# Half-size weight slots with single-piece waits, and block products in three of the layers' input projections

## The reference, cut to what matters

```python
h = layer_norm(concat([meta, x]), ln_emb_g, ln_emb_b)        # 528 rows
for l in range(2):
    proj = h @ w_in[l]      # q,k,v,gate of retention; pool input; q,k,v of attention; forget logits
    mix = concat([retention(...), pool(...), forgetting_attention(...)]) @ w_out[l]
    h = layer_norm(ALPHA * h + mix, ln1_g[l], ln1_b[l])
    y = (silu(h @ w1[l]) * (h @ w3[l])) @ w2[l]              # inner width 2816
    h = layer_norm(ALPHA * h + y, ln2_g[l], ln2_b[l])
return h[16:]
```

## Time and profile before

| what | value |
|---|---|
| median of three runs | 3274.61 us (3264.3, 3274.61, 3277.98) |
| the profiled execution | 3272.24 us, span 3270.1 us |
| mean granted TensorE clock | 0.965 |
| busy share of TensorE, DVE, ACT | 94%, 36%, 17% |
| the two layers | from about 1735 us to the end |
| DMA busy share in slices of 82 us after 1735 us | 2 to 5 tenths |
| TensorE busy in the same slices | 8 to 9 tenths or more |

### The profile page before, as it was taken

One profiled execution on the slowest core, in us unless ns is written; L12 is line 12 of the kernel. 1 busy time (PEld: TensorE's weight loads), 2 busy tenths in 40 slices (PEclk: granted clock), 3 DMA queues, 4 the chain that ended last, 5 costly groups with the idle time before them and its releaser, 6 DMA issues.

```text
span 3270.1 us, 52738 instructions
## 1 busy us (share of the span) xinstructions
PE 3080.4 (94%) x22521; PEld 1730.5 (53%) x22521; DVE 1163.1 (36%) x2350; ACT 545.3 (17%) x1133; POOL 47.4 (1%) x58
## 2 busy tenths in 40 slices
PE   9878989799999999999989999998999989999999
PEld 3355545233333334333445668573786648675766
DVE  1633355222222222232363452527044342435131
ACT  1332320111111111111122221130112100130000
POOL 0000002000000000000010000000000000000000
PEclk9878989899999999999989999999999999999999
DMA  9800125899999999999853333324333243343442
GB/s 400 351 1 30 49 84 220 319 409 407 410 402 408 407 406 406 405 409 408 356 234 125 118 132 113 144 109 162 148 121 147 103 193 129 116 162 116 180 158 100
DMA packets 97467, 743.71 MB, mean 227 GB/s; under 512 B 11128, under 2 KB 38336, under 8 KB 57552
## 3 DMA queue, kind: packets, MB, share of 16 engines
q1 hardware_dynamic: 58768, 687.49, 53.1%
q10 hardware_dynamic: 32624, 30.52, 2.9%
q0 software_dynamic: 5968, 24.14, 1.9%
HBM read 674.98 MB, written 67.13 MB: 227 GB/s over the span
## 4 chain that ended last, share of the span: by engine, by line
PE 55%; DMA 26%; DVE 4%; ACT 2%; issue 1%; ACTq 1%; POOL 1%; DVEq 0%
DMA arena<-x_sorted 24%; PE psum L1648 19%; PE psum L1632 10%; PE psum L1577 5%; PE psum L1281 3%; PE psum L1588 3%; PE psum L1356 2%; PE psum L839 1%; PE psum L1392 1%; ACTq L597 1%; PE psum L1233 1%; PE psum L857 1%; PE psum L1679 1%; PE psum L1448 1%; DMA x_sorted<-arena 1%
## 5 line engine op out<-in xcount | busy, mean ns | idle before, releaser
L1281 PE MATMUL psum<-weight_ring,arena 128*32 128x512 f32 x6192 | 677.5, 595 | 42.8 <-DVE arena L2936 42.1
L1648 PE MATMUL psum<-arena,weight_ring 128*128 128x256 f32 (+1 forms) x2816 | 636.8, 385 | 5.7 <-ACT arena L2291 5.7
L1648 PEld LDWEIGHTS psum<-arena,weight_ring 128*128 128x128 f32 x2816 | 529.4, 190 | 102.2 <-issue 11.9
L1281 PEld LDWEIGHTS psum<-weight_ring,arena 128*32 128x32 f32 x6192 | 199.9, 110 | 500.7 <-issue 458.4
L1356 PE MATMUL psum<-weight_ring,arena 128*32 128x256 f32 x6144 | 338.2, 380 | 0.0
L1356 PEld LDWEIGHTS psum<-weight_ring,arena 128*32 128x32 f32 x6144 | 196.6, 110 | 153.0 <-issue 26.8
L2958 DVE STREAM_TRANSPOSE arena<-arena 128x384 f32<-128x384 f32 x32 | 18.6, 580 | 632.8 <-DMA arena<-x_sorted 632.8
L1632 PE MATMUL psum<-weight_ring 128*128 128x512 f32 x468 | 206.7, 600 | 10.1 <-DMA weight_ring<-weights 8.0
L3273 DVE TENSOR_TENSOR weight_ring<-weight_ring,psum 128x256 f32<-128x256 f32 (+1 forms) x88 | 37.4, 425 | 423.2 <-PE psum L1648 420.5
L1577 PE MATMUL psum<-weight_ring,arena 128*128 128x512 f32 (+2 forms) x512 | 175.0, 500 | 3.1 <-ACT arena L2291 3.1
L1632 PEld LDWEIGHTS psum<-weight_ring 128*128 128x128 f32 x468 | 89.5, 192 | 123.7 <-issue 118.6
(11 more groups left out here) (446 smaller groups left out, 2678.5 us busy)
## 6 DMA issues: line engine op xcount, KB each, us to landing
weight_ring<-exp_gu SPq DMA_DIRECT2D x129, 2048.0 KB, 11.6
weight_ring<-weights SPq DMA_DIRECT2D x104, 2048.0 KB, 7.9
weight_ring<-exp_down SPq DMA_DIRECT2D x64, 2048.0 KB, 11.1
x_sorted<-arena SPq DMA_DIRECT2D x2, 10752.0 KB
arena<-x_sorted ACTq DMA_DIRECT2D x132, 96.0 KB, 22.2
y_sorted<-arena ACTq DMA_DIRECT2D x128, 96.0 KB, 17.4
y_sorted<-arena SPq DMA_DIRECT2D x2, 5632.0 KB, 39.4
y_sorted<-arena SPq DMA_DIRECT2D x2, 5120.0 KB, 37.8
```

The costliest lines, as they stand in the source:

```text
L1281: mm = pe.matmul(psum[j * GROUP:(j + 1) * GROUP, g, :], xg[:, k // 4, g, k % 4 * GROUP:(k % 4 + 1) * GROUP], w[:, kk, j * 512:(j + 1) * 51 ...
L1648: mm = pe.matmul(bank[:, 0:b - a], w[:, k, col:col + P], h2_t[:, k, a:b], start=(k == 0), stop=(k == KT - 1))
```

## The change

The four slots of 2 MB become eight half slots of 1 MB. A piece of the projections, of `mix` and of `feed_up` takes two halves, a down chunk is now six pieces of one half each (three for the first 512 columns, three for the second, in an own input `down2`). A class `Piece` carries its landing wait and its releases, a class `Stream` finds which earlier pieces lay in the same halves. Block products wait on TensorE for single pieces inside p1 and release the second-column pieces after p3 and the last weight sums, the first-column pieces after p5.
The projections (0, A), (1, A) and (1, B) do row chunks 0 and 1 of the two full tiles as one block product, behind the meta items. ACT copies p1, p7, p6 and p3 to `u2`, DVE adds p2, p4 and p5, and ACT applies Silu to the gates in place at the end. The sums of rows go to the other half's columns of `h2_t`, so that the rows are kept.
The norms after `mix` become a generator (`mid_norms`): one tile at a time, between sums of the product or behind features. The norms after the second `feed_down` are centred for all tiles first and then scaled. The double steps of attention become fewer, and the steps inside `feed_down` go. ACT takes the last root of down (1, A) after the last turned tile instead of between the two.

```diff
+HALF_SLOTS, HALF = 2 * LAYER_SLOTS, PIECE // 2
-EARLY_STEPS = range(7, 18)
-DOUBLE_STEPS = dict(A=(4, 5, 6, 7, 8, 12), B=(5, 6, 7))
-DOWN_STEPS = (0, 2)
+EARLY_STEPS = range(4, 15)
+DOUBLE_STEPS = dict(A=(4, 5, 6), B=())
...
+class Stream:
+    def ask(self, source, size):
+        slot = self.at % HALF_SLOTS
+        self.arrived[slot] += 16
+        piece = Piece(source, self.at, size, self.ring[:, slot * HALF:(slot + size) * HALF], (self.landed[slot], self.arrived[slot]))
+        self.pieces.append(piece)
+        self.at += size
+        return piece
...
+        def rows_in_products(l, x):
+            return (l, x) != (0, "B")
...
-            for n in range(len(ROW_CHUNKS)):
+            if rows_in_products(l, x):
+                if x == "A":
+                    yield "meta", 0, 0
+                    yield "meta", 1, 0
+                yield "products", 1, WHOLE[x][-1]
+            for n in range(2 if rows_in_products(l, x) else 0, len(ROW_CHUNKS)):
...
             # TensorE, project
+                    if kind == "products":
+                        products(("product", l, x), KT // 2, left_blocks_kept(x), mix_blocks(ws), [ws[0]] * 2, [ws[1]], None, ("p1", "p7", "p6", "p3"))
+                        main.number["rows", l, x, n, t] = main.number["product", l, x, "p5"]
+                        continue
...
             # TensorE, products
+                        if n == 0 and name == "p1":
+                            first[part].wait(pe)
+                        if q == pairs - 1 and name == "p2" and left_whole is not None:
+                            left_whole(pe)
...
+                    main.ship(mm, (*key, name), "a" if name in copied else "v")
+                    if name == "p3":
+                        for piece in second:
+                            piece.free = [main.done(), (right_ready, parts + 4 * len(right))]
+                for piece in first:
+                    piece.free = [main.done()]
...
             # TensorE, feed_down
-                pe.wait_ge(*main.drained_of(("up", l, x, f1 - 1)))
-                ws = [weights(l, W_DOWN + 3 * c + n) for n in range(3)]
+                    second, first = ([down_weights(l, c, half, n) for n in range(DOWN_PIECES // 2)] for half in (1, 0))
...
+                    pe.wait_ge(*main.drained_of(("up", l, x, f1 - 2)))
+                    products(("down", l, x, c), pairs, left_blocks(ff_t, pairs, x, a), down_blocks(halves, c), first, second, last_ready)
...
             # ACT
+            def product_rows(l, x):
+                t1, t2 = WHOLE[x]
+                for name, t, at in (("p1", t1, 0), ("p7", t2, 512), ("p6", t2, 0), ("p3", t1, 512)):
+                    bank = main.take(act, ("product", l, x, name))
+                    A.did(act.copy(u2[:, t, at:at + 512], bank), main.drained["a"])
+                act.wait_ge(*main.drained_of(("product", l, x, "p5")))
+                gates = u2[:, t1:t2 + 1, U_G:2 * 512]
+                A.did(act.activation(gates, gates, ACT.Silu))
...
-                turn_rows("mid", 1, "B", (last,))
+                turn_rows("mid", 1, "B", (None, last))
...
             # DVE, project
+                    if kind == "products":
+                        ws = mark["rows", l, x]
+                        for w in ws:
+                            w.wait(dve)
+                        for before in range(2 if x == "A" else 0):
+                            main.take(dve, ("meta", l, x, before, 0))
+                        dve.wait_ge(*main.drained_of(("start", l, WHOLE[x][-1], 1)))
+                        products(("product", l, x), left_blocks_kept(x), mix_blocks(ws), x, u2,
+                                 copied_by=dict(p2="p1", p4="p6", p5="p3"), between=norms)
...
             # DVE, products
                 right_sums((0, 1), (1, 1), ALU.subtract, (0, 1))
-                V.did(dve.tensor_tensor(a21, a11, a21, ALU.subtract), left_ready)
+                left_sums("s3", "a11", ALU.subtract, "a21")
                 V.settle_other(left_ready)
-                V.did(dve.tensor_tensor(s2, a22, a21, ALU.subtract), left_ready)
+                left_sums("s2", "a22", ALU.subtract, "s3")
+                each(between)
                 gather("p1", t1, lo, scale, main.drained["v"])
...
             # DVE, mix and feed_down
+            def mid_norms(l, x):
                 for t in rows_of(l, x):
                     norm_rows(V, h2[0:SIZE[t], t, :], t, ln_par2, sem("mid_ready"), SIZE[t], first_half=(t == 0))
+                    yield
...
-                        for t in rows_of(l, x):
-                            norm_scaled(norm_centered(t), sem("layer_start"), parts)
+                        for both in [norm_centered(t) for t in rows_of(l, x)]:
+                            norm_scaled(both, sem("layer_start"), parts)
...
             # DVE, layers
-                project(0, "B", items=(SPLIT_B, 99))
+                project(0, "B", items=(SPLIT_B, 99), norms=mid_norms(0, "A"))
...
-                project(1, "A")
+                norms = mid_norms(0, "B")
+                each(norms)
+                project(1, "A", norms=norms)
...
-                project(1, "B")
+                norms = mid_norms(1, "A")
+                each(norms)
+                project(1, "B", norms=norms)
```

More of the change, by code:

```diff
@@ L414, in take, with __init__, wait, before @@
         return self.psum[:, self.at(self.taken - 1), :]
+class Piece:
+    def __init__(self, source, at, size, flat, landed):
+        self.source, self.at, self.size, self.flat, self.landed, self.free = source, at, size, flat, landed, []
+        self.rows = flat.rearrange("p (k n) -> p k n", n=512)
+    def wait(self, engine):
+        engine.wait_ge(*self.landed)
+class Stream:
+    def __init__(self, ring, landed):
+        self.ring, self.landed, self.arrived = ring, landed, [0] * HALF_SLOTS
+        self.pieces, self.at = [], 0
+    def ask(self, source, size):
+        slot = self.at % HALF_SLOTS
+        assert slot + size <= HALF_SLOTS
+        self.arrived[slot] += 16
[3 more added lines that the diff above has]
+        return piece
+    def before(self, piece):
+        places = {p % HALF_SLOTS for p in range(piece.at, piece.at + piece.size)}
+        found = []
+        for earlier in reversed(self.pieces[:self.pieces.index(piece)]):
+            own = {p % HALF_SLOTS for p in range(earlier.at, earlier.at + earlier.size)}
+            if own & places:
+                found.insert(0, earlier)
+                places -= own
+        return found
 def build(nc, io):
@@ L1548, in project @@
                 a, b = SPAN[x]
-                for number, (kind, n, t) in enumerate(project_items(x)):
+                ws = [weights(l, half) for half in range(2)] if rows_in_products(l, x) else []
+                mark["rows", l, x] = ws
+                for number, (kind, n, t) in enumerate(project_items(l, x)):
                     if not items[0] <= number < items[1]:
@@ L1597, in mix @@
                 pe.wait_ge(*fox_outs.drained_of(("fox", l, x, 3)))
-                ws, ats = zip(*(weights(l, W_OUT + half) for half in range(2)))
-                mark["mix", l, x] = ats
+                ws = [weights(l, W_OUT + half) for half in range(2)]
+                mark["mix", l, x] = ws
                 if 0 in rows_of(l, x):
@@ L1602, in mix @@
                         bank = main.bank(pe)
+                        ws[half].wait(pe)
                         for k in range(KT):
@@ L1640, in feed_up @@
                     if f % 2 == 0:
-                        w, at = weights(l, W_FFN + f // 2)
+                        piece = weights(l, W_FFN + f // 2)
+                        piece.wait(pe)
+                        w = piece.rows
                     for kind, by, col in (("gate", "a", 0), ("up", "v", 256)):
@@ L1676, in feed_down @@
                     for f in range(f1 - f0):
-                        w = views[f // 4][:, f % 4, :]
+                        piece = halves[half][f // 4]
+                        if f % 4 == 0:
+                            piece.wait(pe)
                         first, last = f == 0, f == f1 - f0 - 1
-                        mm = pe.matmul(bank, ff_t[:, f, OFF[t] - a:OFF[t] - a + P], w[:, half * 512:(half + 1) * 512], start=first, stop=last)
+                        mm = pe.matmul(bank, ff_t[:, f, OFF[t] - a:OFF[t] - a + P], piece.rows[:, f % 4, :], start=first, stop=last)
                     main.ship(mm, ("down", l, c, half, t), "v")
-                for _, at in ws:
-                    piece_free[at] = main.done()
+                    for piece in halves[half]:
+                        piece.free = [main.done()]
             def feed(l, x, steps):
@@ L3308, in feed_down @@
                     a, b = span(l, x)
-                    ats, pairs, scale = mark["down", l, x, c], (FF_CHUNKS[c][1] - FF_CHUNKS[c][0]) // 2, 1.0 if c else ALPHA2
```

(3 more changed lines are left out.)

196 lines of the change are left out of this document (107 added, 89 removed).

## The result

The changed kernel took 3234.92 us (median of 4 runs, 3233.68 to 3238.11) against 3275.12 us before (4 runs). The ratio is 0.989, 95% interval 0.9866 to 0.9915. The profiled execution took 3233.68 us, with a span of 3231.6. Timed twice more, on other chips, it gave 0.991 and 0.9895. The forecast was 3245, within 3236 to 3255 if its mechanism held and 3229 to 3262 over all.

The account below looks back on a forecast made before the run. In the layers TensorE is busy nine tenths or more, so its own work and gaps count. Terms sum to -28.6 us: 3272.2 profiled becomes 3243.6, or 3246.0 as median; forecast 3245, range 3229 to 3262.

Parts of the forecast that it names:

- Projection products: Three projections: 56 records instead of 64 in chunks 0 and 1, 10.4 us saved; 3.8 us lost again in (1, A).
- Mix (0, B): Weights arrive in time, but p7 waits 8.9 us for vector-engine norms and sums: 1.1 us slower.
- Mix (1, A): Same as mix (0, B) with two tiles of norms, a wait of 4.8 us: 4.0 us gained.
- Down (1, A): Second chunk: half pieces land 5.3 and 7.8 us after the mix, p1 waits 3.6 and 0.8 us: 4.5 us gained.
- Interleaved norms in (0, B): Projection (0, B): one norm per feature lets drains come in time, so the feed starts earlier: 2.4 us gained.
- Pace: Attention: fewer double steps put softmax units one feature pair apart, removing the softmax scaling waits: 5.0 us gained.
- down starts: Start of down projections: six TensorE waits of 0.5 us go: 3.2 us gained.
- Turned rows after down (1, A): Last root put behind the tile copies: 2.6 us of wait and 1.4 of clock loss saved, 4.0 us gained.
- Rival A: The three 8 us transfer waits and their clock loss vanish, 31.9 us instead of 7.4: 3220 us; chance 0.08.
- Rival C: Vector engine's first round so late that TensorE stands at p7 in each projection; from 12 us delay, 3275 and more; chance 0.03.
- D: Second halves' release is held up and softmax waits reappear at feed ends; only down starts and products gain: 3262; chance 0.07.

Follow-up runs that it names:

- the whole release: The changed kernel with half slots kept, but each product waiting for all its pieces before p1 and freeing all after p5: 3248.06 us, ratio 0.9956.
- the experiment: The changed kernel with the old table of attention double steps restored: 3240.63 us, ratio 0.9933.
- the short norms: Norms after layer 0's two down projections scale only 16 of 1024 columns: in the kernel before 3264.37 us (1.0), in the changed kernel 3215.33 us (0.9861).

## Why the prediction was right

The forecast held (3245 forecast, 3234.9 measured, inside 3229 to 3262) and so did the mechanism. The size was less good: 3234.9 lies 1 us below the 3236 to 3255 that the theory had given as its own, and two terms left their bounds. Step by step, in the same two profiles:

- Projection products, -10.4 + 3.8. 56 records in 24.30, 26.00 and 20.87 + 3.70 us. The scalar wait at p2 of (1, A) came at 2.67 us, predicted 2.8. The clock stayed at 1.00 behind it, so 1.0 us was priced too much. Without the products the stages take 8.2 us more; predicted 6.6, which held the 1.0 too many.
- Mix (0, B), +1.1: measured +0.8 in these two profiles (1.6 against the whole release). The wait at p7 was 9.16, predicted 8.9. It came out of the vector engine's list in time; the list of waits could not show it.
- Mix (1, A), -4.0: measured -4.1, with a wait of 4.94 (4.8).
- Down (1, A), -4.5 (bounds 2 and 6.5): measured -6.9, outside the bounds. The waits were 3.18 and 0.57 (3.6 and 0.8). The halves were requested from 2962.19 on, right behind the mix's end at 2962.16, and took 4.8 and 7.0 us from issue to landing. They were in use at 2967.05 and 2969.60, which is 4.9 and 7.4 us after the mix: predicted 5.3 and 7.8. The Trainium skill, page "DMA: Bandwidth & Descriptors", section "Anatomy of one DMA — SWDGE (gpsimd) path", fits its 2.0 us plus bytes over 436 GB/s to transfers that GpSimd issues, and these come from the sync queue. Read as one transfer after the other it makes 4.4 and 8.8 us, an estimate from that page; the trace bears out the overlap instead. Most of what the term missed is the clock: I had put 1.7 us for it, and none was lost.
- Interleaved norms in (0, B), -2.4: the feed starts 2.9 us sooner behind the mix's end (19.3 us behind it, 22.3 before). The wait of 3.06 us is gone with its low clock, and 1.75 us stand at the turned rows.
- Pace, -5.0, and down starts, -3.2: all these waits went, and the first came back alone in the experiment. The sum gave the pace alone the 5.0; by the whole release, the early release is needed for it too.
- Turned rows after down (1, A), -4.0 (bounds 2 and 5): the wait fell by 2.85 us and the feed took 3.0 us less, 5.9 in all, outside the bounds. I had assumed that 1.7 us of low clock would stay behind the shorter gap, and it didn't.

So 6 of the 10 us beyond the forecast are clock: 1.7 at the start of projection (0, A), slow before and not after, 1.0 at p2 of (1, A), 1.7 in down (1, A) and 1.7 behind the last turn, where I charged what a similar gap had cost before. The other 4 are small terms, none above 1.4. The losses are not gone for good. After a transfer wait of 3.1 to 3.4 us in down (1, A) the clock fell in five of the eleven profiles that have it, among them the one without products and the one with the old pace, but in none of the changed kernel's own three; whether it also comes and goes there within one program is not shown. By the medians of its three timings the gain is 40, 29 and 32 us. None is below the forecast of 28.6, and two are within 4 us of it, so the size of the excess is within what the timings scatter.

Rival A needed the norms to be free; the short norms show that they aren't. Rival C's 12 us of delay in each projection never came. D's release was not held up.

## What to carry to other kernels

When a transfer wait is the largest in the list, write out what the other engines do beside it: here 8.0 us of waiting for weights became 9.2 of waiting for norms. An instruction that is moved later also moves what waits for its buffer; look for the transfer that it releases before counting the gain. And price the clock loss behind a gap of 2 to 3.4 us as a chance, not as a sum.

## What I had not expected of the hardware

- After the same gap of 1.97 us at the start of projection (0, A), the first matmuls ran at 1.2 GHz in seven of the 14 profiles and at 2.4 in the other seven. One program did both: 128 small records took 3.69 us in one profile of the changed kernel and 5.36 in the next. A wait of 3.18 us was harmless at clock 1.00 (2967 to 2977) and one of 3.32 us, in the kernel with short norms, was not. Gaps of 7.8 us and more were followed by a low clock in every profile. The Trainium skill, page "TensorE: Matmul & The Clock Gate", section "Part 1: The HAM clock gate (the "warmup" mystery)", says of a kernel's start that the count of slow matmuls varies from run to run of one kernel; the two rows show the like in the middle of one.
- The 1 MB transfer of norm parameters, broadcast to all partitions from GpSimd's queue, took 4.6 to 12.8 us to land, and the 264 KB ones of the scalar queue 10.5 and 18.6 (medians of two windows). The slow ones had weight pieces moving beside them; no run here separates size from company.
